# Tail sums of stick-breaking attention as float32r high and low parts in two passes, on one Trainium2 core

## What is computed

```
for blk in range(seq // SB_BLOCK):            # 4 blocks of 128 queries, 16 heads of 64
    z = einsum('bhtd,bhsd->bhts', qf[:, :, t0:t1], kf[:, :, :t1])
    causal = arange(t1)[None, :] < (t0 + arange(SB_BLOCK))[:, None]
    log_1mb = where(causal, log_sigmoid(-z), 0.0)
    tail = cumsum(log_1mb, axis=3, reverse=True)
    w = where(causal, exp(z + tail), 0.0)
    outs.append(einsum('bhts,bhsd->bhtd', w, vf[:, :, :t1]))
```

## Time and profile before

| what | us |
|---|---|
| median of 3 runs (2972.52 to 2974.84) | 2973.14 |
| the profiled execution: its own time | 2973.76 |
| its span in the profile | 2972.0 |
| PE busy in the span | 2735.0 (92%) |
| DVE busy | 1661.8 (56%) |
| ACT busy | 937.6 (32%) |
| POOL busy | 1350.8 (45%) |
| granted PE clock, mean | 0.966 of full speed |

### The profile page before, as it was taken

How to read it: one execution, slowest core, us unless ns; L and a number is a source line. 1 busy time by engine, 2 the same in 40 slices (tenths; PEclk the granted TensorE clock), 3 DMA queues, 4 the chain that set the end, 5 groups by cost and what they waited for, 6 DMA issues and landing times.

```text
span 2972.0 us, 32441 instructions
## 1 busy us (share of the span) xinstructions
PE 2735.0 (92%) x12074; PEld 2069.3 (70%) x12074; DVE 1661.8 (56%) x3130; ACT 937.6 (32%) x1682; POOL 1350.8 (45%) x995
## 2 busy tenths in 40 slices
PE   7989999899998999999896789999999999989944
PEld 6856888777888678888775668888888754434411
DVE  1032145575144354420306639999996999856686
ACT  3275334665243332222336223111112940000001
POOL 3433543665455134444333226444445954444465
PEclk9999999999999999999998889999999999999977
DMA  4311233332243146653220037999999369999998
GB/s 158 103 53 36 85 100 87 120 106 74 97 139 124 49 133 201 198 163 100 80 85 29 22 107 254 376 389 392 376 390 407 104 246 381 391 411 409 409 382 296
DMA packets 221245, 599.11 MB, mean 202 GB/s; under 512 B 24465, under 2 KB 49314, under 8 KB 220578
## 3 DMA queue, kind: packets, MB, share of 16 engines
q1 hardware_dynamic: 137312, 301.22, 29.7%
q0 software_dynamic: 75968, 275.81, 24.5%
q10 hardware_dynamic: 7810, 20.02, 2.0%
HBM read 585.36 MB, written 7.41 MB: 199 GB/s over the span
## 4 chain that ended last, share of the span: by engine, by line
PE 70%; DVE 12%; DMA 10%; issue 3%; POOL 3%; ACT 3%; SPq 0%; DVEq 0%; ACTq 0%; POOLq 0%
PE ps L1796 15%; PE ps L1293 13%; PE ps L1295 13%; PE ps L1294 13%; DMA rows<-in_v,expert 5%; DMA rows<-in_u,expert 5%; DVE ps L2497 3%; PE ps L1259 1%; POOL wlo L1095 1%; PE ps L1391 1%; PE ps L1824 1%; POOL rows L1204 1%; DVE rows L2483 1%; PE ps L1813 1%; PE ps L1478 1%
## 5 line engine op out<-in xcount | busy, mean ns | idle before, releaser
L1095 POOL TENSOR_TENSOR wlo<-wraw,whi 128x1024 fp32r<-128x1024 f32 x258 | 627.5, 2444 | 869.2 <-ACT whi L581 868.8
L581 ACT ACTIVATE whi<-wraw 128x1024 fp32r<-128x1024 f32 x258 | 269.2, 1058 | 708.8 <-PE ps L1295 594.6
L1293 PE MATMUL ps<-hhi,whi 128*128 128x512 f32 x1096 | 432.9, 395 | 19.4 <-DVE hlo L1948 5.3
L1836 PE MATMUL ps<-stream,hg 128*128 128x512 f32 x1024 | 442.5, 595 | 8.2 <-DMA stream<-in_v 8.2
L1796 PE MATMUL ps<-haff,stream 128*128 128x256 f32 x2048 | 444.1, 380 | 2.2 <-ACT stg L999 2.2
L1295 PE MATMUL ps<-hhi,wlo 128*128 128x512 f32 x1096 | 429.9, 392 | 0.0
L1294 PE MATMUL ps<-hlo,whi 128*128 128x512 f32 x1096 | 429.8, 392 | 0.0
L1796 PEld LDWEIGHTS ps<-haff,stream 128*128 128x128 f32 x2048 | 390.1, 191 | 55.7 <-ACT stg L999 2.4
L1204 POOL DMA_INDIRECT rows<-in_u,expert x256 | 264.7, 1034 | 267.5 <-DVE hid L2483 141.2
L1836 PEld LDWEIGHTS ps<-stream,hg 128*128 128x128 f32 x1024 | 195.3, 191 | 255.3 <-issue 245.5
L1204 POOL DMA_INDIRECT rows<-in_v,expert x256 | 248.1, 969 | 260.5 <-DVE ps L2497 123.2
(11 more groups left out here) (465 smaller groups left out, 4376.4 us busy)
## 6 DMA issues: line engine op xcount, KB each, us to landing
stream<-in_ut SPq DMA_DIRECT2D x128, 512.0 KB
stream<-in_v SPq DMA_DIRECT2D x128, 512.0 KB
wraw<-in_w_in SPq DMA_DIRECT2D x96, 512.0 KB
wraw<-in_w_ada SPq DMA_DIRECT2D x48, 512.0 KB
wraw<-in_w_gu SPq DMA_DIRECT2D x88, 256.0 KB
wraw<-in_w_down SPq DMA_DIRECT2D x22, 512.0 KB
decs<-acs_kept ACTq DMA_DIRECT2D x16, 512.0 KB, 3.7
wraw<-in_w_br_ssm SPq DMA_DIRECT2D x16, 512.0 KB
```

The lines of the kernel that those rows point to most:

```text
L581: act.activation(whi[:, n % WSLOTS, 0:kn, :], wraw[:, n % WSLOTS, 0:kn, :], ACT.Copy).then_inc(w_hi, 1)
L1095: pool.tensor_tensor(wlo[:, n % WSLOTS, 0:kn, :], wraw[:, n % WSLOTS, 0:kn, :], whi[:, n % WSLOTS, 0:kn, :].bitcast(F32), ALU.subtract).th ...
L1293: pe.matmul(dst, lh, rh, start=k == 0, stop=False)
L1836: ins = pe.matmul(ps[:, 2 * i + half, :], hg[:, n, P * i:P * i + P], stream[j][:, 4 * half:4 * half + 4, :], start=n == 0, stop=n == NKEYS ...
```

## The change

The nine float32 products of `tails` are replaced by products on float32r operands. POOL copies the masked `sb_p` into `sb_hi` (1280 columns, float32r) behind its two selects. DVE subtracts `sb_hi` from `sb_p` into `sb_lo` (1280 columns, in the place of `sb_p`), copies the sums of later blocks to `later_hi` (384 columns) and subtracts again for `later_lo`. The two constant matrices are copied once into `sb_c` as float32r. PE runs the seven products on `sb_hi`, the same seven on `sb_lo` and four on the later sums, each pass behind its own wait. `sb_hi` lies in the place of `sb_l`, so log_part(h) now waits for `tail_ready` of head h-2 instead of `sp_ready` of head h-2.

```
             def log_part(h):
                 act.wait_ge(z_ready, 2 * h + 2)
                 if h >= 2:
-                    act.wait_ge(sp_ready, 2 * (h - 2) + 1)
+                    act.wait_ge(tail_ready, 2 * (h - 2) + 2)
...
             def mask_logs(h):

-                pool.wait_ge(sp_ready, 2 * h + 1)
+                pool.wait_ge(sp_ready, 3 * h + 1)
...
+                pool.wait_ge(sp_masked, 3 * h + 2)
+                pool.tensor_copy(sb_hi[:, h % 2, :], sb_p[:, h % 2, :]).then_inc(sp_masked, 1)
...
             def tails(h):

-                pe.wait_ge(sp_masked, 2 * h + 2)
-                for b in (2, 1, 3, 0):
...
+                for n_half, p in enumerate((sb_hi[:, h % 2, :], sb_lo[:, h % 2, :])):
+                    own = [p[:, 0:512], p[:, 512:896], p[:, 1024:1280], p[:, 896:1024]]
+                    next_block = {2: own[3], 1: own[2][:, 0:P], 0: own[1][:, 0:P]}
+                    if n_half == 0:
+                        pe.wait_ge(sp_masked, 3 * h + 3)
+                    else:
+                        pe.wait_ge(sp_ready, 3 * h + 2)
+                    for b in (2, 1, 3, 0):
+                        bank, off, n = place[b]
+                        pe.matmul(ps[:, 3 * (h % 2) + bank, off:off + n], sb_c[:, 0:P], own[b], start=False, stop=n_half == 1 and b == 3, skip_group_check=True)
+                    for b in (2, 1, 0):
+                        bank, off, n = place[b]
+                        pe.matmul(ps[:, 3 * (h % 2) + bank, off + P:off + 2 * P], sb_c[:, P:2 * P], next_block[b],
+                                  start=False, stop=n_half == 1, skip_group_check=True)
+                pe.wait_ge(sp_ready, 3 * h + 3)
+                for b, c0, c1 in ((1, 0, P), (0, P, 3 * P)):
                     bank, off, n = place[b]
...
+                    for sums in (later_hi[:, h % 2, c0:c1], later_low(h)[:, c0:c1]):
+                        ins = pe.matmul(ps[:, 3 * (h % 2) + bank, off + 2 * P:off + 2 * P + c1 - c0], sb_c[:, P:2 * P], sums,
                                         start=False, stop=True, skip_group_check=True)
+                    ins.then_inc(tail_ready, 1)
...
             def later_blocks(h):

                 p, later = sb_p[:, h % 2, :], later_sums(h)
-                v.wait_ge(sp_masked, 2 * h + 2)
+                v.wait_ge(sp_masked, 3 * h + 2)
                 v.tensor_tensor(later[:, P:2 * P], p[:, 640:768], p[:, 1024:1152], ALU.add)
                 link(v.tensor_tensor(later[:, 0:P], p[:, 1152:1280], p[:, 896:1024], ALU.add))
-                v.tensor_tensor(later[:, 2 * P:3 * P], p[:, 768:896], later[:, 0:P], ALU.add).then_inc(sp_ready, 1)
+                link(v.tensor_tensor(later[:, 2 * P:3 * P], p[:, 768:896], later[:, 0:P], ALU.add))
+                v.wait_ge(sp_masked, 3 * h + 3)
+                v.tensor_tensor(sb_lo[:, h % 2, :], p, sb_hi[:, h % 2, :].bitcast(F32), ALU.subtract).then_inc(sp_ready, 1)
+                link(v.tensor_copy(later_hi[:, h % 2, :], later))
+                v.tensor_tensor(later_low(h), later, later_hi[:, h % 2, :].bitcast(F32), ALU.subtract).then_inc(sp_ready, 1)
...
+            v.tensor_copy(sb_c[:], cst[:, C_NEGGE:C_NEGGE + 2 * P])
             softplus(0)
```

More of the change, by code:

```diff
@@ L261, in build_program @@
         sb_x = at("sb_x", XRES, 8, [P, 2, 2, T])
+        sb_hi = at("sb_hi", TT, 0, [P, 2, 1280], F32R)
+        sb_lo = at("sb_lo", TT, 10, [P, 2, 1280], F32R)
+        later_hi = at("later_hi", XRES, 5, [P, 2, 384], F32R)
+        later_lo = (at("later_lo0", M, 12, [P, 2, 384], F32R), at("later_lo1", A, 16, [P, 2, 512], F32R))
+        sb_c = at("sb_c", M, 15, [P, 2 * P], F32R)
         sb_r = (at("sb_r0", M, 12, [P, 2, 384]), at("sb_r1", A, 16, [P, 2, 512]))
@@ L502, in later_sums, with later_low @@
             return sb_r[0][:, h, :] if h < 2 else sb_r[1][:, h % 2, 0:384]
+        def later_low(h):
+            return later_lo[0][:, h, :] if h < 2 else later_lo[1][:, h % 2, 0:384]
         def scores_of(h, first, n):
@@ L1382, in tails @@
             def tails(h):
[L1384 to L1387, removed]
-                pe.wait_ge(sp_masked, 2 * h + 2)
-                for b in (2, 1, 3, 0):
-                    bank, off, n = place[b]
-                    pe.matmul(ps[:, 3 * (h % 2) + bank, off:off + n], cst[:, C_NEGGE:C_NEGGE + P], own[b], start=False, stop=b == 3, skip_group_check=True)
@@ L1398, in tails @@
+                pe.wait_ge(sp_ready, 3 * h + 3)
+                for b, c0, c1 in ((1, 0, P), (0, P, 3 * P)):
+                    bank, off, n = place[b]
+                    for sums in (later_hi[:, h % 2, c0:c1], later_low(h)[:, c0:c1]):
+                        ins = pe.matmul(ps[:, 3 * (h % 2) + bank, off + 2 * P:off + 2 * P + c1 - c0], sb_c[:, P:2 * P], sums,
                                         start=False, stop=True, skip_group_check=True)
-                    if b < 2:
-                        ins.then_inc(tail_ready, 1)
+                    ins.then_inc(tail_ready, 1)
```

## The result

| | before | after |
|---|---|---|
| median | 2972.83 us (4 runs, 2971.23 to 2974.84) | 3004.34 us (4 runs, 3000.35 to 3006.64) |
| the profiled execution: its own time, its span | 2973.76, 2972.0 | 3006.64, 3004.9 |
| granted PE clock, mean | 0.966 | 0.957 |

The changed kernel is slower: the ratio of the times is 1.0105, with the interval [1.0089, 1.0121]. The kernel became 31.5 us longer where 12.9 were forecast. The time lies in the attention stage. From the first instruction of scores(0) to the first product of the next projection it took 114.3 us before (156.34 to 270.66) and takes 146.6 us after (157.65 to 304.27), 32.3 us more. In front of the stage the profile after is 1.3 us later; PE's clock stood there at 0.66 and not at 0.83 in one early stretch (20 to 30 us) that the change does not touch.

What follows compares the result with a forecast made beforehand. PE was taken to bound the kernel at 6.40 us a head, other engines 0.06 us below. 13 periods of 0.85 us more (11.1) plus 1.8 at the front gave 12.9 us, 2986.7 us; range 2977 to 3006.

Steps and rivals of the forecast that it cites:

- PE bounds before: Middle heads of the attention stage: PE alone sets the period, 6.40 us, hiding the other engines with 0.06 us to spare.
- The terms of the path: From softplus to the last tails products: POOL copy 1.32 us, DVE subtraction 1.48, copy of 384 columns 0.40, last subtraction 0.56.
- L: String of other engines from the end of scores(h+1) to the start of tails(h+1): 6.34 us before, 8.07 forecast after.
- D: Time from the start of a head's tails to its end: forecast 3.7 us, only 2.4 of it work.
- The half rule: P = (L + D + 2.71) / 2 once PE waits before tails: savings in D and additions to L count half.
- P: Period of one head in the attention stage: forecast 7.25 us, 0.85 more than 6.40.
- Turns between DVE and POOL: Around POOL's copy: DVE additions and POOL alternate by instruction; two additions precede the copy, the third stands behind it.
- the clock stays: Attention stage: outputs and scores keep 1.23 and 1.48 us and passes full speed; the sum has no clock term.
- the falling clock: Rival, chance 0.13: PE idles between works, half of the heads run at 1.2 GHz, 13 us on top, 2999 us.
- the rival's price: Falling clock's cost: outputs and scores 2.7 us more, half into P; with the longer last pass about 1.8 x 7 = 13 us.
- A slow copy: Rival, chance 0.17: POOL's copy runs at its other operations' rate, 2.95 us, end 37 us later, 3011 us.
- No slower: Rival, chance 0.17 within 0.2%, 0.03 faster: additions run beside the copy, turns cost nothing, P = 6.6 us, 2977 us.

Runs made afterwards that it cites:

- e5: Kernel before, with ACT computing ln(1 + exp(z)) in two operations straight into `sb_p` and DVE's softplus gone; 2964.32 us, ratio 0.9986 to before.
- e10: Changed kernel with 9 PE products of zeros a head in the wait before the high pass only; 2986.78 us, ratio 1.0060 to before.
- e11: Changed kernel with 7 PE products of zeros a head in the wait before the low pass only; 2987.98 us, ratio 1.0065 to before.
- e2: Kernel before, still float32, with POOL's copy of 1280 columns put ahead of the tails and read by nobody; 2981.18 us, ratio 1.0049 to before.
- e1: Changed kernel with 16 PE products of zeros a head, 9 before the high pass and 7 before the low pass; 2983.64 us, ratio 1.0052 to before.
- e6: Changed kernel with ACT computing ln(1 + exp(z)) straight into `sb_p` and DVE's softplus gone; 2964.97 us, ratio 0.9985 to before.
- e3: Changed kernel with the mask added by PE products, DVE making both parts, and no POOL selects or DVE additions; 2977.26 us, ratio 1.0028 to before.
- e7: e4 with 13 PE products of zeros a head before the high pass; 2968.66 us, ratio 1.0000 to before.
- e8: e6 with DVE's `rest_heads` called one head later; 2960.86 us, ratio 0.9971 to before.
- e4: Changed kernel without the low parts: no subtraction into `sb_lo`, no low pass, no low later products; 2979.71 us, ratio 1.0038 to before.

## Why the prediction was wrong

**What held.** *PE bounds before* (6.40 us a head): e5 shows it. *The terms of the path*: the copy took 1.36 us (forecast 1.32), the subtraction 1.49 (1.48), the copy of 384 columns 0.35 (0.40), and `later_lo` 0.56. A pass at full speed takes 0.64 + 0.28 = 0.92 us (0.97), and the four later products 0.51 (0.46), so a float32r product of 128 columns steps by 0.11 us, the value taken and not its upper end of 0.22. L is 241.40 - 233.55 = 7.85 us (8.07), and D at full speed, with its wait, 2.20 + 1.58 = 3.78 (3.7). *The half rule*: with these, P = (7.85 + 3.78 + 2.71) / 2 = 7.17; e10 and e11 measured 7.19 to 7.29 against the forecast 7.25, and e2 half of its copy. e1's 7.29 is no test of it, since PE is the chain there. *Turns between DVE and POOL*: the second addition is held by the copy. The groups by form of after give the means over the 16 heads (busy us, mean ns of one, idle before):
```profile
L1139 POOL CAST sb_hi<-sb_p 128x1280 fp32r<-128x1280 f32 x16 | 21.8, 1363 | 1.0
L2006 DVE TENSOR_TENSOR sb_r<-sb_p 128x128 f32<-128x128 f32 x16 | 20.7, 1291 | 0.0
...
L2005 DVE TENSOR_TENSOR sb_r<-sb_p 128x128 f32<-128x128 f32 x16 | 4.9, 309 | 8.7 <-POOL sb_p L1136 8.7
```
Without an addition beside it the copy takes 1.25 us (e6 at 215.74, where DVE is waiting). The Trainium skill, page "SBUF — State Buffer", section "Who interferes with whom", says that a DVE instruction with two SBUF inputs and a GpSimd instruction that reads SBUF exclude each other by a lock; by that rule, the trace agrees, 1291 ns for 0.29 us of work. The Trainium skill, page "GPSIMD Engine Reference", section "Elementwise — side-by-side cycle accounting", would make the copy about 1.1 us, an estimate from its 1.03 cycles an element; the measurement decides, 1.36 us in after and 1.25 with nothing beside it.

**What failed: "the clock stays".** The forecast sum has outputs and scores at 2.71 us and both passes at full speed in every head, and so no term for the clock; the runs show 17.9 us of stage for it (e1 against after). The prediction had the falling clock as a rival at 0.13, and drew the range up to 3006 to take it in; the 3004.34 us lie just below that end. The case was the rival's, on top of the forecast chain. The step rested on the earlier trace rows, 7.8 of 10 us busy at 1.00. That is a share with the waits anywhere in it; here two waits of 1.48 and 1.01 us stand in the same head, with only the 1.2 us of the high pass between them. From that row "stays" could not be read, and the row beside it, 5.77 of 10 us at 0.66, could as well have been the nearer one.

**What was mis-sized: the rival's price.** It had the right condition (half of the heads at 1.2 GHz) and 13 us for it; the measured price is 17.9 us. From the start of the low pass to that of outputs the slow head takes 2.96 us (226.34 to 229.30) and the fast one 1.58 (234.58 to 236.16), 1.38 us more. Outputs cost 1.10 us more, scores 0.44. The rule itself stands. Over two heads 2P = L + D + outputs + scores = 7.85 + 5.16 + 2.33 + 1.92 = 17.26 us, and high passes start at 224.14 and 241.40, 17.26 us apart. At full speed the same sum is 14.3. The 2.9 us come once in every two heads, so it is about 2.9 x 13 / 2 = 19 us. The prediction halved the price by the rule and then took it for half of the heads only, which counts the half twice. Before halving it had 2.7 us for outputs and scores, where 1.5 were measured, since the clock is back before the scores end, and about 0.9 for the longer pass, where 1.38 were measured. With these three errors against each other, it is partly luck that the time lies inside the range.

**Smaller misses.** The high pass comes 0.3 us earlier than computed, since the copy gets in ahead of the second addition and not behind it. The waits are not 0.8 us in each head but 1.48 in every second one, with DVE idle for 3.70 us before softplus there. And PE waits 0.93 us before scores in the heads between, for ACT's weights behind its logarithm. It adds nothing to the period of after, because it lies inside L; e3 shows that this loop, at 6.9 us, would be the next bound. Whether it helps to bring the clock down is not shown.

**The other rivals.** A slow copy is refuted by 1363 ns. "No slower" is refuted by e2, where the copy on the path costs 11 us by itself at an unchanged clock, and by e10 and e11, at 7.19 to 7.29 us a head where it had 6.6.

**What stays open.** Which of the waits counts for more, and how long a wait the clock bears: filling either set in e10 and e11 also shortened or removed the other waits, and one head of after (201.17) had all of them and kept its full clock. That the clock has this effect in after itself is shown by filling the waits, not by holding the clock, which cannot be tried.

## What to carry to other kernels

Before a cheaper form of the bounding engine's work goes in, compute the loop through the other engines: where the work on PE covers a string of the same length, saving on PE brings nothing, and what is added to the string costs half. Then price every new wait of PE twice, once as time and once as clock, at the instructions that follow it; if the waits can't be avoided, zero products in them that nobody waits for can be worth more than they cost (17.9 us of stage here). Size them so that they end before the wait does: in e1 they filled PE to the last and set its pace themselves, and in e7 they stand in the chain. And look on each queue for what stands ahead of the new work without being needed for it: moving one such call by a head took the stage from 110.5 us (e6) to 105.6 (e8), the first version in which the change seems to pay (e5, without the change, has 108.7).

## What was not expected of the hardware

- With waits of 0.93, 1.48 and 1.01 us around every second head the mean granted clock of a 100-us stretch was 0.79; with one set of zero products it was 0.93 or 0.97, and 1.00 from 180 us on.
- More work for PE made the kernel faster: 16 products a head take after from 31.5 to 13.9 us above the kernel before measured beside it, and 13 a head take e4 from 9.9 above it to 0.3 below.
- A one-input copy to float32r takes 1363 ns for 1280 columns on POOL, and 1.25 us where DVE stands still. A DVE addition of 128 columns with two SBUF inputs that starts beside it takes 1291 ns for 0.29 us of work, while the one 0.2 us ahead of it takes 0.31.
